# Sixteen expert pairs in another order: the largest pair two places later, and the last pair's rows copied by two engines

## What is computed

```python
h = rms_norm(x, g_mix[l])
x = x + mixer(h, ...)                      # convolution branch and sparse attention
h = rms_norm(x, g_ffn[l])
x = x + hier_moe(h, ...)                   # 4 groups x 8 experts
return rms_norm(x, g_final)

# hier_moe: each token goes to its best group, and there to its best two experts
a = jnp.einsum('td,edf->tef', ht, wg)      # D 1024 -> FF 256
b = jnp.einsum('td,edf->tef', ht, wu)
return jnp.einsum('tef,efd->td', jax.nn.silu(a) * b * c[:, :, None], wd)
```

## Time and profile before

| | us |
|---|---|
| median of 3 runs (665.07 to 667.53) | 665.1 |
| profiled execution | 666.17 |
| its span, first to last instruction | 664.0 |
| PE busy in the span | 581.1 (88%) |
| first tile of the expert phase starts | 391.61 |

### The profile page before, as it was taken

How to read it: one execution, slowest core, us unless ns; L and a number is a source line. 1 busy time by engine, 2 the same in 40 slices (tenths; PEclk the granted TensorE clock), 3 DMA queues, 4 the chain that set the end, 5 groups by cost and what they waited for, 6 DMA issues and landing times.

```text
span 664.0 us, 12478 instructions
## 1 busy us (share of the span) xinstructions
PE 581.1 (88%) x4371; PEld 383.1 (58%) x4376; DVE 344.2 (52%) x853; ACT 258.2 (39%) x446; POOL 295.8 (45%) x466
## 2 busy tenths in 40 slices
PE   3899999999999999999999957899989849696882
PEld 2587788877666676877888423444444424243440
DVE  4417999999979896369132782122112101111146
ACT  6344333244755675544322103333433413233232
POOL 5343444469996322346530035454544433425230
PEclk9899999999999999999999787999999989999996
DMA  9132632622222024033069989999699999999863
GB/s 294 22 111 65 203 114 64 137 64 65 64 64 65 0 84 172 0 127 131 28 254 342 395 331 387 409 407 397 224 406 409 408 408 409 406 400 399 322 266 126
DMA packets 64606, 149.04 MB, mean 224 GB/s; under 512 B 14372, under 2 KB 30756, under 8 KB 64574
## 3 DMA queue, kind: packets, MB, share of 16 engines
q1 hardware_dynamic: 59150, 139.90, 56.9%
q0 software_dynamic: 5280, 8.22, 3.5%
q10 hardware_dynamic: 144, 0.52, 0.3%
HBM read 145.11 MB, written 12.60 MB: 238 GB/s over the span
## 4 chain that ended last, share of the span: by engine, by line
PE 55%; DVE 20%; SPq 9%; DMA 6%; issue 4%; ACT 4%; POOL 1%; POOLq 0%; DVEq 0%; ACTq 0%
PE bank L704 26%; PE bank L1018 10%; SPq L429 7%; PE bank L1035 5%; DMA region<-in_w_e_up 5%; DVE bm L1468 5%; DVE m L1467 4%; DVE conv_buf L1459 3%; PE bank L782 2%; SPq L439 2%; PE bank L985 2%; PE bank L815 2%; PE bank L932 1%; PE bank L803 1%; PE bank L961 1%
## 5 line engine op out<-in xcount | busy, mean ns | idle before, releaser
L704 PE MATMUL bank<-h_hi,w_part 128*128 128x512 f32 (+1 forms) x528 | 174.5, 400 | 3.2 <-DVE h_lo L1417 1.7
L557 POOL TENSOR_TENSOR w_part<-region,w_part 128x1024 fp32r<-128x1024 f32 (+1 forms) x52 | 109.8, 2113 | 146.5 <-ACT w_part L1105 146.5
L704 PEld LDWEIGHTS bank<-h_hi,w_part 128*128 128x128 f32 (+1 forms) x528 | 98.3, 186 | 31.0 <-issue 8.0
L1018 PE MATMUL bank<-region,kT 128*32 128x256 f32 x1536 | 93.0, 396 | 19.4 <-DMA region<-in_w_e_up 14.7
L1794 DVE TENSOR_TENSOR mask_b<-mask_b,bank 128x128 f32<-128x128 f32 x30 | 8.6, 288 | 184.7 <-ACT mask_b L1368 184.7
L704 PE MATMUL bank<-h_lo,w_part 128*128 128x512 f32 (+1 forms) x264 | 103.5, 392 | 0.0
L1018 PEld LDWEIGHTS bank<-region,kT 128*32 128x32 f32 x1536 | 55.3, 115 | 64.7 <-issue 41.7
L1105 ACT ACTIVATE w_part<-region 128x1024 fp32r<-128x1024 f32 (+1 forms) x52 | 48.0, 925 | 106.2 <-PE bank L704 106.0
L607 POOL TENSOR_TENSOR carrier<-mhalf 128x1 f32<-128x1 f32 x183 | 33.5, 201 | 119.4 <-ACT qT L1375 105.5
L1502 DVE SCALAR_TENSOR_TENSOR bank<-glu,cv,bank 128x256 f32<-128x256 f32 x196 | 78.6, 478 | 0.0
L1035 PE MATMUL bank<-region,mask_b 128*32 128x512 f32 x384 | 47.9, 617 | 11.0 <-DVE mask_b L1797 11.0
(11 more groups left out here) (288 smaller groups left out, 897.6 us busy)
## 6 DMA issues: line engine op xcount, KB each, us to landing
region<-in_w_e_down SPq DMA_DIRECT2D x22, 1024.0 KB, 16.1
region<-in_w_e_gate SPq DMA_DIRECT2D x44, 512.0 KB, 10.0
region<-in_w_e_up SPq DMA_DIRECT2D x44, 512.0 KB, 11.7
region<-in_w_in SPq DMA_DIRECT2D x16, 1024.0 KB, 6.1
conv_buf<-in_w_e_down SPq DMA_DIRECT2D x10, 1024.0 KB, 18.4
gates<-in_w_e_gate SPq DMA_DIRECT2D x20, 512.0 KB
gates<-in_w_e_up SPq DMA_DIRECT2D x20, 512.0 KB
region<-in_w_out SPq DMA_DIRECT2D x2, 2048.0 KB, 7.8
```

The costliest lines, as they stand in the source:

```text
L557: g.tensor_tensor(unit_part(u, 1), unit_raw(u), unit_part(u, 0).bitcast(F32), ALU.subtract)\
L704: last = mm(out_, a_parts[p], b_parts[q], start=start and x_ == 0, stop=stop and x_ == 2)
L1018: last = mm(bank[0][32 * c:32 * c + 32, 0:FF], xTs[:, k, at_:at_ + 32], w_gu[slot][:, e, :, half, k, j * P:(j + 1) * P], start=(half == 0 ...
```

## The change

It has three parts. `place_rank` puts the ranks at other places. On TensorE, 26 warming matmuls run instead of 14, the two table values of place 0 are read ahead of the table products, and the first round of the loop over three places is written out. At the end, the four transposes of `col_w` go ahead of place 15's tiles and ScalarE's copy of them ahead of its work for the last tile; VectorE takes two of the last tile's four copies, and two of its late adds move ahead of a scaling.

```diff
-        place_rank = list(range(SETS)) + [SETS + r for r in (5, 0, 6, 7, 1, 8, 9, 2, 10, 3, 11, 4, 12)]
+        place_rank = list(range(SETS)) + [SETS + r for r in (5, 6, 7, 0, 8, 9, 1, 10, 2, 3, 11, 4, 12)]
...
             transpose_tile(0)
-            keep_warm(14)
-
-            pe.wait_ge(S["oh_ready"], 1)
-            for cc in range(2 * TB):
-                for c in range(4):
-                    last = mm(bank[4][32 * c:32 * c + 32, 0:2 * MAXT], ohlo[:, cc, :],
-                              ohv[:, cc, :, c // 2 * MAXT:(c // 2 + 1) * MAXT], start=(cc == 0),
-                              stop=(cc == 2 * TB - 1))
-            last.then_inc(S["tab_mm"], 1)
+            keep_warm(26)
+
+            def table_products():
+
+                pe.wait_ge(S["oh_ready"], 1)
+                for cc in range(2 * TB):
+                    for c in range(4):
+                        last = mm(bank[4][32 * c:32 * c + 32, 0:2 * MAXT], ohlo[:, cc, :],
+                                  ohv[:, cc, :, c // 2 * MAXT:(c // 2 + 1) * MAXT], start=(cc == 0),
+                                  stop=(cc == 2 * TB - 1))
+                last.then_inc(S["tab_mm"], 1)
...
                 end = pe.value_load(tab[0:1, n + 1:n + 2] if isinstance(n, int) else tab[0:1, bass.ds(n + 1, 1)],
                                     min_val=1, max_val=MAXT - 1)
+                if isinstance(n, int) and n == 0:
+                    table_products()
                 with pe.Fori(first, end) as t:
...
-            with pe.Fori(0, PAIRS // SETS) as i:
+            pe.wait_ge(S["tab_ready"], 1)
+            for slot in range(SETS):
+                pair_tiles(slot, slot, 0)
+            with pe.Fori(1, PAIRS // SETS) as i:
                 for slot in range(SETS):
                     pair_tiles(SETS * i + slot, slot, i)
-            for n in range(PAIRS // SETS * SETS, PAIRS):
-                pair_tiles(n, n % SETS, n // SETS)
-
-            early = pe.value_load(tab[0:1, PAIRS + 1:PAIRS + 2], min_val=PAIRS - 2, max_val=MAXT - 3)
             pe.wait_ge(S["col_ready"], 1)
             for b in range(TB):
                 last = tr(bank[5][:, b * P:(b + 1) * P], col_w[:, b, :], ident[:])
             last.then_inc(S["place_mm"], 1)
+            for n in range(PAIRS // SETS * SETS, PAIRS):
+                pair_tiles(n, n % SETS, n // SETS)
+
+            early = pe.value_load(tab[0:1, PAIRS + 1:PAIRS + 2], min_val=PAIRS - 2, max_val=MAXT - 3)
...
             pe.wait_ge(S["yev_a"], early + 3)
+            pe.wait_ge(S["late_ev"], 1)
             pe.wait_ge(S["place_ev"], 1)
...
+                if u:
+                    act.wait_ge(S["place_mm"], 1)
+                    a(place, bank[5][:], ACT.Copy).then_inc(S["place_ev"], 1)
                 hidden_gate(early + u)
-                for n in range(2):
+                for n in range(2 - u):
                     for e in range(2):
...
-            act.wait_ge(S["place_mm"], 1)
-            a(place, bank[5][:], ACT.Copy).then_inc(S["place_ev"], 1)
...
-            for b in range(2):
-                add_row(b, 0)
+            add_row(0, 0)
+            dve.wait_ge(S["y_mm"], early + 2)
+            for e in range(2):
+                at_ = 64 + 32 * e
+                last = v.tensor_copy(late[at_:at_ + 32, 1, :], bank[2][32 * (2 * e + 1):32 * (2 * e + 1) + 32, :])
+            last.then_inc(S["late_ev"], 1)
+            add_row(1, 0)
...
             mean_square(2, 1)
+            for k in range(4, 6):
+                add_late(k)
             scale_out(1, whole)
-            for k in range(4, 8):
+            for k in range(6, 8):
                 add_late(k)
```

More of the change, by code:

```diff
@@ L298, in build @@
             rt_mm exp_in exp_out m_ready rank_mm oh_ready tab_mm tab_ready gu_half gu_mm silu_g hid_ready
-            hidT_mm hidT_ev y_mm yev_a xg_mm xtev_a xtev_v idx_copy y_add hits_ready first_mm diagw_ready col_ready late_ready place_mm place_ev late_mm late_add o_ready dve_chain pool_chain
+            hidT_mm hidT_ev y_mm yev_a xg_mm xtev_a xtev_v idx_copy y_add hits_ready first_mm diagw_ready late_ev col_ready late_ready place_mm place_ev late_mm late_add o_ready dve_chain pool_chain
             ys_free rows_ready xg_ready sidx_copy conv_pool order_ready""".split()
```

## The result

The changed kernel takes 659.58 us (median of 20 runs, 657.92 to 664.23), the kernel before, run beside it, 666.11 (median of 20, 663.16 to 668.73). The ratio is 0.992, with a 95% interval of 0.9902 to 0.9937: 0.8% faster, 5.3 us by the ratio. The forecast was 656.0 and its range 653 to 661.

What follows compares the result with a forecast made beforehand. The prediction took the weight stream as the bound from 526 us on. Hole 6.0, start 2.0 and end 1.2 sum to 9.2 us, taking the profiled 666.17 to 657.0, 656.0 as median; range 653 to 661.

Steps and rivals of the forecast that it cites:

- rival 3: Hole moves to place 9 if the pair of six starts late or early-finished engines count: 660 to 664 us; chance 0.16.
- all three parts work: Table, start and end all gain as forecast: 656.0 us, own range 653 to 658.3; chance 0.55.
- three signs of being wrong: New hole before place 9's load; three pairs slower than 54.5 us once the stream never rests; returned rows staying put.
- TensorE's chain from place 6 to 15: TensorE's time from place 6's start to place 15's: 159.2 us, leaving it no slack against the stream.
- The slow tile: Place 6's first tile, after a wait of about 10 us, starts at low clock and takes 1.7 us more.
- So the queue is not dry, by 2 to 3 us, and the hole is gone: Place 9's load is issued 38 us after place 6's weights land, while queued loads last 40.4 us.
- Hole 6.0: Removing the weight stream's hole at 464 to 476 us gains 6.0 us: 60.5 for three pairs less the neighbour's 54.5.
- bytes are the same: In the expert phase, the new order of pairs leaves the bytes moved unchanged; no size given.
- Start 2.0: At the expert phase's start, an earlier first tile at full clock puts the stream 2.0 us ahead.
- Against it: At the start, late table products delay place 3's down load, engines run dry 2 to 3 us; could cost 0.6.
- End 1.2: After the weight stream, reordered copies and late adds gain 1.2 us together; bounds 0 and 1.5.
- The small gain at GpSimd: At the end, GpSimd's first square root comes earlier, so VectorE's wait of 0.57 us goes.

Runs made afterwards that it cites:

- e1: The kernel before with only the new `place_rank` table: 663.36 us, ratio 0.9951 to the kernel before.
- e7: The whole change with the two-tile pair of place 14 moved to place 5: 660.73 us, ratio 0.9926 to the kernel before.
- e12: The whole change with a two-tile pair at place 5 and two idle matmuls ahead of the first weighted row: 662.76 us, ratio 0.9956 to the kernel before.
- e8: The whole change with 14 warming matmuls instead of 26: 661.08 us, ratio 0.9921 to the kernel before.
- e3: The kernel before with only the end changed (transposes, two VectorE copies, two late adds): 666.02 us, ratio 0.9993 to the kernel before.
- e6: The whole change with the pair of six tiles at place 5 instead of 6: 661.60 us, ratio 0.9937 to the kernel before.
- e11: The whole change with two idle matmuls ahead of the first weighted row: 660.43 us, ratio 0.9909 to the kernel before.
- e4: The whole change again, run on the same chip as its single parts: 662.02 us, ratio 0.9925 to the kernel before.
- e5: The whole change with four idle matmuls ahead of the first weighted row: 662.01 us, ratio 0.9946 to the kernel before.
- e9: The kernel before with no token rows gathered (output left wrong): 657.04 us, ratio 0.9873 to the kernel before.

## Why the prediction was right, and where it was not

**What bounds it, the direction, the range.** Right, the size with some luck: 659.6 lies in the range only by its upper part, which was there for rival 3; "all three parts work" had 653 to 658.3. Two of the three signs of being wrong came: a new hole ahead of place 9's load, and three pairs (places 9 to 12) that took 55.3 us, more than 54.5. The stream sets the end before and after, and the table moves TensorE's wait from behind the pair of six to ahead of it. The forecast of 3 and 10 us at places 5 and 6 came as 3.55 and 9.49; TensorE's chain from place 6 to 15, forecast at 159.2, took 162.1 less the two waits of 1.52 and 1.99, 158.6. The slow tile cost 2.1 (5.78 against 3.66), forecast 1.7. A tile was slow behind a wait in five places here (5.78, 5.35 in e1, 5.27 in e7, 6.26 in e12, and 5.34); the Trainium skill, "TensorE: Matmul & The Clock Gate", section "HAM oscillation — how this bites in real kernels", says that a wait for DMA has this effect, and these rows agree, though place 5's tile kept 3.66 behind 3.55 us.

**The failed step: "So the queue is not dry, by 2 to 3 us, and the hole is gone".** Rival 3 came true in part, by its second condition, "the engines that had finished early count". The arithmetic of the step was good for the last DMA engine: place 9 was issued at 38.7 behind place 6's tile, forecast 38, and place 6's, 7's and 8's loads were to last until 40.4 behind it, 504.7. But the pace of 17.3 us per pair is that of landings, and a load has landed when the slowest of 16 has done its part. Place 8's down load, the last in the queue, was issued from 482.11 on; its last semaphore event stands at 504.8, as forecast, but its first at 491.0, and the mean share was 0.72 from 496 to 500 already. Some engines had emptied their queues by then, most of them from 500 to 504 us, where the share was 0.37. The hole is 4.5 us in place of none.

**"Hole 6.0" was 3.3 to 3.4.** That is what the table brought by itself: 0.49% in e1, and 3.4 us from the table products to place 15 (240.7 to 237.3). The forecast took its 6.0 from one stretch, 60.5 against 54.5, as if all of the excess were the hole. The stretch did fall by more than that, 6.3 us (60.4 to 54.1; 6.5 in e1), but only 2.3 of it is hole. The rest is bytes that moved on: "bytes are the same" holds for the whole, not for each stretch. With the pair of six two places later, three more tiles stand at places 9 to 15 (15 instead of 12), and behind place 9 there are 1.24 MB more of gathers and scatters and 0.84 MB more of weights, the latter because the quick engines' lead at place 9 was smaller (6.0 us against 11.0) and at place 15 the same. At 0.408 MB/us these are 5.1 us; the stretch grew by 4.0, its mean rate being 398 GB/s instead of 394.

**"Start 2.0" was 0.6 to 1.3.** The first tile ran at full clock and started 0.52 behind the start of the products instead of 2.43, and place 3's load was issued 3.3 us sooner behind them. Place 3 landed 3.8 us sooner, place 4 only 1.1: the down load's issue did not move, and the DMA engines ran short at 404 to 412 us (0.74, 0.87), 1.7 us in the place of 2.8 before. This is the case weighed under "Against it", and e8 shows that the warming, one of this part's three edits, is worth nothing that can be measured. The fear that the reads would delay the products was wrong: they wait for VectorE (0.82), not for the reads.

**"End 1.2" is right in size where the clock stays up.** The end took 33.0, 33.1, 33.1, 32.7 and 32.6 us in e3, e6, e7, e8 and e11, against 34.0 before; in the changed kernel's profile and in e4 the clock fell ahead of the first weighted row and it took 34.4 and 34.7. VectorE's copy was 0.70, forecast 0.67. The small gain at GpSimd did not come in the changed kernel's profile, where VectorE's wait of 0.57 is as long as before; in e3, e6, e8 and e11 that wait is gone. From the add of block 3 to the end it was 17.8 us, 0.9 less than 18.7 (17.2 to 17.3 in those four), but that add came 16.6 behind place 15's landing instead of 15.4. The forecast had no such case. And in the times the end's gain can't be told from nothing: e3, the end alone, is 0.9993 with 1 inside its interval. The transposes that were moved stood between the last tile and the weighted rows and shortened TensorE's pause there; without them it waits 1.95 instead of 1.28 us, as the kernel before has it there:

```profile
637.12 0.66 PE L1049 MATMUL bank<-ident,mask 128*128 128x128 f32 x4
639.05 1.95 PE L1061 MATMUL bank<-region,glu 128*128 128x512 f32 x4 [1.28 <-DMA region<-expert_rows]
```

But e3 waited 2.40 and e6 2.33 and kept the full clock, so the length of that wait alone does not decide it, and e6 and e8 have the changed kernel's end word for word. What decides it stays open. The idle products of e5 and e11 kept the clock up in one profile each.

**The sum.** Forecast 9.2. From the table products to the end the profiles show 4.3 (the table of stretches): 4.7 up to place 15, where 8.0 was forecast for hole and start, and 0.4 lost at the end, where 1.2 was to be gained. The ratio says 5.3, the medians 6.5. What the forecast lacks is thus first the part of the hole that stayed, 4.5 us, then half of the start, then the clock at the end, in those executions that it hits; how many these are, single profiles don't tell.

## What to carry to other kernels

A queue fed by many DMA engines runs dry when the quick ones do, not when the last load lands: to see whether a queue bridges a pause, take the mean share's fall ahead of the last landing, not the landings' pace. When work is moved later, count what rides with it (gathers, scatters) in the stretch behind it, and read the gain at the end of the stream: here a stretch that fell by 6.3 us held 2.3 of gain and 3.9 of bytes that only went later. And an end that waits for small things can pay for its clock: an edit that takes TensorE's filler work out of a pause may cost more than the filler did, as in two profiles here (in those of e3, e6 and e8 the clock stayed up).

## What was unexpected of the hardware

The DMA engines that share each load drift far apart, and rows drive them on. From the first to the last event of a down load it was 3 us at place 0 and 14 to 15 at places 13 to 15, in the kernel before and in the changed one; a hole brings them together (from 12.5 at place 6 to 6.7 at place 7 before, from 13.7 at place 8 to 6.0 at place 9 changed). Without gathers the mean over places 4 to 14 is 7.9 and 7.2 us instead of 11.9 and 10.6.

Leaving gathers out shortened the last stretch by more than their bytes. In the changed kernel 1.65 MB less in q0 (3.74 to 2.09) and 0.34 MB less of weights are 4.9 us at 0.408 MB/us; the stretch fell by 6.9. In the kernel before, 0.74 MB less rows and 0.35 MB more weights are 1.0 us; it fell by 3.6. That is 2.0 and 2.6 us more than the bytes. A part of it is that the quick engines are out of weights ahead of the last landing: the share was 0.65 from 624 to 628 us before, with place 15 landing at 629.9, where e9 had 0.91 from 616 to 620 and landed at 621.1. That a row's byte costs more than a weight's does not follow: the mean rate of the stretch was 394 and 398 GB/s with gathers and 404 and 406 without, but e7 and e12, with gathers, had 406 and 407. These are single profiles of each.

TensorE's low clock showed in rows of very different size: 5.27 to 6.26 us for a tile of 3.66, and 2.79 to 3.23 for a row of 1.88, with pauses ahead of it from 1.95 to 9.49 us, while pauses of 2.33 and 2.40 ahead of a row, and of 3.55 ahead of a tile, left it at full clock.
